# Second block, first layer of the compressing network: upper and lower gathered blocks side by side as one stationary operand of 128 columns

## What is computed

```python
def compress_blocks(t, pos_emb, w1, b1, w2, b2):
    B, G, T, dh = t.shape
    nc = n_cmp_blocks(T)
    idx = np.arange(nc)[:, None] * CMP_STRIDE + np.arange(CMP_BLOCK)[None, :]
    blocks = t[:, :, idx, :] + pos_emb
    flat = blocks.reshape(B, G, nc, CMP_BLOCK * dh)
    return jax.nn.gelu(flat @ w1 + b1) @ w2 + b2
...
    kc = compress_blocks(kc, cmp_pos[0], cmp_w1[0], cmp_b1[0], cmp_w2[0], cmp_b2[0])
    vc = compress_blocks(vc, cmp_pos[1], cmp_w1[1], cmp_b1[1], cmp_w2[1], cmp_b2[1])
```

## Time and profile before

| | us |
|---|---|
| median of 3 runs | 2792.5 |
| lowest, highest | 2792.41, 2792.8 |
| profiled execution | 2789.8 |
| its span | 2787.6 |
| PE busy in the span | 2709.6 (97%), 13505 matmuls |
| DVE busy | 1518.1 (54%) |
| ACT busy | 1141.4 (41%) |
| POOL busy | 204.8 (7%) |
| mean granted clock of TensorE | 0.996 |

### The profile page before, as it was taken

One profiled execution on the slowest core, in us unless ns is written; L12 is line 12 of the kernel. 1 busy time (PEld: TensorE's weight loads), 2 busy tenths in 40 slices (PEclk: granted clock), 3 DMA queues, 4 the chain that ended last, 5 costly groups with the idle time before them and its releaser, 6 DMA issues.

```text
span 2787.6 us, 34775 instructions
## 1 busy us (share of the span) xinstructions
PE 2709.6 (97%) x13505; PEld 2236.5 (80%) x13505; DVE 1518.1 (54%) x2682; ACT 1141.4 (41%) x2056; POOL 204.8 (7%) x314
## 2 busy tenths in 40 slices
PE   8999999999999999999999999999999899999997
PEld 7778888888788888777778888888778788888886
DVE  6756444466564444576766653343667666643433
ACT  3644222236542222355654343232455644342331
POOL 5200000002000000021121000000020211000000
PEclk9999999999999999999999999999999999999999
DMA  4103232221032323332311232333323111323332
GB/s 122 55 27 99 99 99 97 93 85 57 24 102 98 97 94 97 95 92 72 95 46 54 91 98 95 95 98 98 103 65 106 58 54 61 99 93 96 98 99 76
DMA packets 187638, 235.60 MB, mean 85 GB/s; under 512 B 12130, under 2 KB 140612, under 8 KB 187476
## 3 DMA queue, kind: packets, MB, share of 16 engines
q1 hardware_dynamic: 184500, 225.95, 25.8%
q0 software_dynamic: 2256, 5.52, 1.0%
q10 hardware_dynamic: 720, 1.92, 0.2%
HBM read 227.05 MB, written 2.11 MB: 82 GB/s over the span
## 4 chain that ended last, share of the span: by engine, by line
PE 83%; DVE 9%; ACT 4%; issue 3%; POOL 0%; DMA 0%; ACTq 0%; DVEq 0%; SPq 0%
PE bank L650 24%; PE bank L652 24%; PE bank L651 24%; DVE Wl L2203 2%; ACT Wh L1479 2%; PE bank L910 1%; PE bank L855 1%; PE bank L931 1%; PE bank L973 1%; PE bank L1171 1%; PE bank L974 1%; PE bank L932 1%; DVE STT L2517 1%; PE bank L840 1%; PE bank L1373 1%
## 5 line engine op out<-in xcount | busy, mean ns | idle before, releaser
L2203 DVE TENSOR_TENSOR Wl<-RAW,Wh 128x1024 fp32r<-128x1024 f32 (+3 forms) x434 | 510.6, 1200 | 403.2 <-ACT Wh L1479 402.5
L1479 ACT ACTIVATE Wh<-RAW 128x1024 fp32r<-128x1024 f32 (+3 forms) x434 | 437.7, 1032 | 410.9 <-PE bank L652 406.4
L650 PE MATMUL bank<-Hh,Wh 128*128 128x512 f32 (+1 forms) x1104 | 447.1, 405 | 2.2 <-issue 1.4
L652 PE MATMUL bank<-Hh,Wl 128*128 128x512 f32 (+1 forms) x1104 | 432.4, 392 | 0.0
L651 PE MATMUL bank<-Hl,Wh 128*128 128x512 f32 (+1 forms) x1104 | 431.8, 391 | 0.0
L650 PE MATMUL bank<-HA,Wh 128*128 128x512 f32 x704 | 274.2, 390 | 0.0
L652 PE MATMUL bank<-HA,Wl 128*128 128x512 f32 x704 | 273.9, 389 | 0.0
L651 PE MATMUL bank<-HA,Wh 128*128 128x512 f32 x704 | 273.9, 389 | 0.0
L652 PEld LDWEIGHTS bank<-Hh,Wl 128*128 128x128 f32 (+1 forms) x1104 | 206.4, 187 | 46.4
L650 PEld LDWEIGHTS bank<-Hh,Wh 128*128 128x128 f32 (+1 forms) x1104 | 207.0, 188 | 44.0 <-issue 4.1
L650 PE MATMUL bank<-A,Wh 128*128 128x512 f32 x608 | 236.5, 389 | 0.0
(11 more groups left out here) (402 smaller groups left out, 4688.1 us busy)
## 6 DMA issues: line engine op xcount, KB each, us to landing
RAW<-in_w_up_dram SPq DMA_DIRECT2D x108, 512.0 KB, 3.6
RAW<-in_w_down_dram SPq DMA_DIRECT2D x108, 512.0 KB, 3.8
RAW<-in_w_in_dram SPq DMA_DIRECT2D x90, 512.0 KB, 3.5
RAW<-in_w_gate_dram SPq DMA_DIRECT2D x44, 512.0 KB, 3.6
RAW<-in_w_out_dram SPq DMA_DIRECT2D x28, 512.0 KB, 3.8
RAW<-in_cmp_w_dram SPq DMA_DIRECT2D x16, 512.0 KB, 4.0
RAW<-in_w_o_fox_dram SPq DMA_DIRECT2D x8, 512.0 KB, 4.0
RAW<-in_w_o_nsa_dram SPq DMA_DIRECT2D x8, 512.0 KB, 3.4
```

What stands on the lines that cost most here:

```text
L650: pe.matmul(o, sh, mh, start=first, stop=False)
L652: return pe.matmul(o, sl, mh, start=False, stop=last)
L1479: sc.activation(M.Wh[:, v % NHL, 0:n], M.RAW[:, v % NRAW, 0:n], ACT.Copy).then_inc(G.w_hi, 1)
L2203: ve.tensor_tensor(M.Wl[:, v % NRAW, 0:n], M.RAW[:, v % NRAW, 0:n], M.Wh[:, v % NHL, 0:n].bitcast(F32), ALU.subtract).then_inc(G.w_lo, 1)
```

## The change

The two parts of the gathered blocks become one tile: XHL[kv] has 16 slices of 128 columns, the upper part in columns 0 to 63 and the lower part in 64 to 127. ACT and DVE write their halves at a pitch of 128. A slice now takes two matmuls: all 128 columns against the weight's upper part, which puts h.h into partitions 0 to 63 of the bank and lo.h into 64 to 127, and columns 0 to 63 against the weight's lower part, added to partitions 0 to 63. The bank's two halves have to be added: ACT copies the lower partitions to HT as before, but signals a new semaphore hid_a, and DVE, at the second step of `keys_side`, waits for it, adds partitions 64 to 127 to HT and releases the bank. The idle steps behind it are cut to eight, so that the later steps keep their places.

```diff
-        self.XHL = [[area("XHL", [16, 64], w + x, F32R) for x in (0, 1024)] for w in (18432, 2048)]
+        self.XHL = [area("XHL", [16, 128], w, F32R) for w in (18432, 2048)]
...
+        self.hid_a = sem("cmp_hidden_first_half_out")
...
                 for k in range(4):
-                    i = three(b[0:64, 0:256], M.XHL[kv][0][:, k0 + k, :], M.XHL[kv][1][:, k0 + k, :], h[:, k, :], lo[:, k, :],
-                              k0 + k == 0, k0 + k == 15)
+                    x = M.XHL[kv][:, k0 + k, :]
+                    pe.matmul(b[:, 0:256], x, h[:, k, :], start=k0 + k == 0, stop=False, skip_group_check=True)
+                    i = pe.matmul(b[0:64, 0:256], x[:, 0:64], lo[:, k, :], start=False, stop=k0 + k == 15, skip_group_check=True)
                     tick()
...
-                sc.activation(M.XHL[kv][0][:, :, :].rearrange("p a b -> p (a b)"), M.XF[:, :], ACT.Copy).then_inc(*hi.up())
+                sc.activation(M.XHL[kv][:, :, 0:64], M.XF[:, :].rearrange("p (a b) -> p a b", b=64), ACT.Copy).then_inc(*hi.up())
...
-                    sc.activation(M.HT[0:64, :], M.bank[K.of(name)][0:64, 0:256], ACT.Copy).then_inc(*K.empties(name))
+                    sc.activation(M.HT[0:64, :], M.bank[K.of(name)][0:64, 0:256], ACT.Copy).then_inc(G.hid_a, 1)
...
-                flat = [x[:, :, :].rearrange("p a b -> p (a b)") for x in M.XHL[kv]]
-                lower(flat[1], M.XF[:, :], flat[0]).then_inc(G.xf, 1)
+                lower(M.XHL[kv][:, :, 64:128], M.XF[:, :].rearrange("p (a b) -> p a b", b=64), M.XHL[kv][:, :, 0:64]).then_inc(G.xf, 1)
...
         def keys_side(kv):
-            yield from idle(9)
+            yield
+            name = f"hid{l} {kv}"
+            ve.wait_ge(G.hid_a, 2 * l + kv + 1)
+            ve.tensor_tensor(M.HT[0:64, :], M.HT[0:64, :], M.bank[K.of(name)][64:128, 0:256], ALU.add).then_inc(*K.empties(name))
+            yield from idle(8)
```

## The result

The changed kernel takes 2806.4 us (median of 4 runs, 2805.9 to 2807.53); the kernel before, run beside it, 2792.65 us (median of 4). The ratio is 1.0052, with a 95% interval of 1.0039 to 1.0065: slower by some 14 us. The forecast was 2805.5.

What follows compares the result with a forecast made beforehand. A near tie, with DVE and ACT carrying the chain around the changed blocks while PE is nearly always busy. Per layer 4.66 + 0.28 + 1.8 - 0.22 = 6.5 us, 13.0 for both, on 2792.5: 2805.5 us, range 2799 to 2811.

Steps and rivals of the forecast that it cites:

- the stall for kv = 0: HT transposes wait for DVE's add, queued behind KS splits: 5.4 us later, shifting GpSimd's wait by 4.66 us a layer.
- The savings: 64 steps over k save 0.112 us each, 7.2 us of PE time; only 0.22 us a layer reaches the end.
- changing the tiling mode drains the engine: Rival at the alternating 128- and 64-column matmuls: each takes 0.28 us instead of 0.115; 2806 us, chance 0.03.
- The five blocks before 1346.30: Blocks ending before PE's wait for a lower weight part from DVE: their 2.2 us saved only widen that 0.43 us wait.
- the 3.79 from the transposes to the first scores: PE's time from HT transposes to the first scores' last matmul: 4.32 us less a 0.53 us wait that goes away.
- The write of the gathered parts: Gathered blocks written 64 columns at a pitch of 128: 0.28 us a layer for DVE's first lower part, ACT's nothing.
- The clock in the stall: PE idle some 5.5 us before kv=0's transposes: clock falls to 1.2 GHz, 1.8 us lost a layer.
- The add for kv = 1: DVE's 0.42 us add right before the maximum at 1405.90 fits into a 0.58 us wait: costs nothing.
- The bank is not taken again before them.: For kv=1: no one takes the hidden bank before the transposes at 1410.91, so DVE's later release costs nothing.
- had no fall: PE's 2.09 us gap at 1377.27, waiting for GpSimd's scaled scores, showed no fall of the granted clock.
- the granted clock is below 1.00 only after those stalls: Sign for the profile after: lowered clock only after PE's stalls, over 5 us before kv=0's transposes in each layer.
- the rival of a longer low level: Clock stays low longer after the stall, 3.4 us lost a layer or more: 2809 to 2812 us, chance 0.13.

Runs made afterwards that it cites:

- the pair of filled kernels: Unread matmuls before six kinds of PE waits, in the kernel before and in the 128-column kernel with both halves added by PE: 2788.61 and 2789.55 us.
- the filled stall: Changed kernel with twenty unread 512-column matmuls on PE before its wait for DVE's kv=0 add: 2803.51 us, ratio 1.0043 to the kernel before.

## Why the prediction was right, and where it was not

The time, 2805.5 against 2806.4, was right for mostly the right reason: the stall for kv = 0 and the low level in it were forecast as they came. But one term of the sum should have been zero and two were missing. In the profiles the change costs 17 us and not 13. That the medians still agree to 1 us is luck: the runs of the kernel before that the forecast was added to were slower than the profile that it was worked out from.

- **The savings.** The pair steps by 0.117 us, near the 0.115 of the earlier trace rows. Two slices after the change:

```profile
1344.76 0.28 PE L1291 MATMUL bank<-Wh,XHL 128*128 128x256 f32 x1
1344.87 0.28 PE L1292 MATMUL bank<-Wl,XHL 128*64 128x256 f32 x1
1344.99 0.28 PE L1291 MATMUL bank<-Wh,XHL 128*128 128x256 f32 x1
1345.11 0.28 PE L1292 MATMUL bank<-Wl,XHL 128*64 128x256 f32 x1
```

  So nothing is lost between the two widths. The Trainium skill, page "TensorEngine Tiling (Array Packing)", section "Key Properties", says that changing the tiling mode drains the engine. If these widths are two such modes, each switch would have waited for the matmul before it, 0.28 us by the rows, and the trace doesn't agree. That next to nothing of the savings reaches the end was right in kind: 0.11 us a layer came through, by the pair of filled kernels, where I had 0.22.
- **The five blocks before 1346.30.** They went into the wait, which I put at 2.6 us. It is 1.72, and 0.69 more at an earlier wait for the same releaser: 2.41.
- **The stall for kv = 0.** The transposes come 7.21 us behind the wait for Wl instead of 1.81: 5.4 later, as forecast. At GpSimd's wait this makes 4.36 us, not 4.66. The step that was too large is the 3.79 from the transposes to the first scores, which accounts for 0.21 of the 0.30. In the changed kernel with the stall and two waits filled it is 3.58:

```profile
1351.88 0.34 PE L1314 MATMUL bank<-CST,HT 64*128 64x64 f32 x2 [0.91 <-DVE HT L3066]
...
1355.46 0.23 PE L973 MATMUL bank<-CMB,IDB 128*128 128x128 bf16 x1
```

  That the wait for DVE is the cause was shown in three ways: made alone it costs everything, taken away it costs nothing that can be measured, moved forward it costs less.
- **The write of the gathered parts.** I took 0.28 us a layer from VN's rows. It is nothing. DVE's four writes take 1227 ns on average before and 1226 after, ACT's 1061 in both:

```profile
L2251 DVE TENSOR_TENSOR XHL<-XF,XHL 128x1024 fp32r<-128x1024 f32 x4 | 4.9, 1227 | 4.5 <-ACT XHL L1982 4.5
...
L1982 ACT ACTIVATE XHL<-XF 128x1024 fp32r<-128x1024 f32 x4 | 4.2, 1061 | 17.7 <-DVE XF L2972 17.7
```

```profile
L2253 DVE TENSOR_TENSOR XHL<-XF,XHL 128x1024 fp32r<-128x1024 f32 x4 | 4.9, 1226 | 4.5 <-ACT XHL L1984 4.5
...
L1984 ACT ACTIVATE XHL<-XF 128x1024 fp32r<-128x1024 f32 x4 | 4.2, 1061 | 17.7 <-DVE XF L2974 17.7
```

  So the layout is not what makes VN 71 ns slower. VN's row is another operation, with three operands, which is the likely reason. I had both bounds, and took the wrong one.
- **The clock in the stall.** 1.8 forecast, 1.81 measured by the filled stall. That the size fits is in part luck: the low level lasted 6.8 us instead of the 3.6 that I reasoned from, but 3.0 us of it lay where PE had no work.
- **The add for kv = 1.** Here a step failed: "The bank is not taken again before them." It is. The hidden layer of kv = 1 lies in bank 7, and PE takes bank 7 for the transposes of GpSimd's scaled scores 35 rows before it transposes HT. PE's order after the change, with each row's number:

```
6288 L911 MATMUL bank7<-CST_13_61,P1_9_57 128x128 [waits score_exp_normed,bank7_drained]
...
6323 L1308 MATMUL bank4<-CST_13_61,HT_111_159 128x64 [waits bank7_drained,bank4_drained]
```

  Before, ACT's copy had released it long since. Now DVE's add does, and that stands behind a scaled tile's lower part. I had looked at when HT is read and not at when its bank is wanted. It costs 1.14 us a layer by the account (1.28 less 0.14 for the low level from 1403: on its two sides ACT's copies of the weights are 8.87 and 9.00 us later than before). The kernel with this add alone on DVE shows the same 1.14 in its trace.
- **Low stretches behind the waits for GpSimd.** I had written that the 2.09 us gap "had no fall", and taken from it that gaps near 2 us have none. It had none in that one execution, and behind the same gap in a second profile of the kernel before the clock falls. So the sign "the granted clock is below 1.00 only after those stalls" failed. In the profile of after these stretches cost 1.57 us a layer (1.43 and 0.14).

Summed for a layer: 4.36 + 0 + 1.81 + 1.14 + 1.57 = 8.9 with the savings of 0.1 already in it, where the forecast was 6.5. The medians are 13.75 us apart and not 17.7. The profiled execution of the kernel before took 2789.8 us, 2.7 under the median of the runs that I added my differences to (2792.5). Other low stretches in those runs are the likely reason. The clock of those runs is not known, but in the last set of 31 runs of this kernel time goes with it: the 11 with a mean granted clock of 0.996 took 2788.8 us on average, and the five at 0.994 or less 2791.4 to 2796.0. Had I known of the add for kv = 1 and nothing of the stretches, I would have said 2808. By its trace the case nearer to what happened is the rival of a longer low level: 13.6 us of it a layer in place of the 3.6 that I took.

## What to carry to other kernels

When a release moves from one engine's instruction to another's, ask two things of the new one: what stands ahead of it in its own queue, and who next takes each thing that it releases, the PSUM bank as well as the data. Matmuls saved ahead of a wait on another engine only lengthen that wait, here by some 2 us a layer; one dependency put into an engine that lags by 5 us cost some fifty times what all the saved matmuls brought to the end (6.17 against 0.11 us a layer). And where runs differ by a microsecond or two, look through the granted clock of every stretch before comparing two profiles: here one stretch was as dear as the effect in question.

## What was not expected of the hardware

- TensorE's low level came in stretches of 3.4 or 6.8 us. There are 75 in the 14 traces (the level at the start and after the last matmul aside), and each has a wait of 1.59 us or more in it or just ahead of it. The same wait had it in one execution and not in another. A stretch of 3.4 us on the chain cost 1.4 to 1.7 us, but that from 1403 only 0.14. The 6.8 us of the stall cost 1.81. What decides between the two outcomes stays open; kernels with saved matmuls had the low level more often.
- Filling a wait with unread matmuls keeps the clock up at that place (5.55 us of stall with 4.7 us filled; five waits of 1.65 to 2.15 us), and the runs draw together (2788.4 to 2791.2 in ten). The gain over the kernel before was 1.9 us, within the error.
- A write of 1024 words a partition at twice the pitch, 64 words at a time, costs DVE and ACT nothing (1226 and 1061 ns, against 1227 and 1061 without gaps).
- An fp32 product of HT with 64 columns of the identity, over 128 partitions, takes 0.2 us (the trace records it as two matmuls), where the transpose over 64 partitions takes 0.13.
